# Residual-stream update and its norm statistics moved between engines, and seven PSUM banks in turn, in a two-block transformer kernel

## The reference, cut to what matters

```
for layer in range(DEPTH):
    h = h + 0.5 * rmsnorm_2(swiglu(rmsnorm_2(h, g[0]), ...), g[1])
    hn = rmsnorm_2(h, g[2])
    mix = gla_mixer(hn, ...) or swa_mixer(hn, ...)
    h = h + rmsnorm_2(mix, g[3])
    h = h + 0.5 * rmsnorm_2(swiglu(rmsnorm_2(h, g[4]), ...), g[5])
    if layer == 0: k_sh, v_sh = shared_kv(h, kv_norm, w_kv, cos, sin)
```

## Time and profile before

| | us |
|---|---|
| median of 3 runs | 1949.22 |
| lowest and highest run | 1944.98, 1959.04 |
| profiled execution, its own time | 1958.64 |
| span in its profile | 1956.8 |
| TensorE busy | 1870.8 (96% of the span) |
| VectorE busy | 1270.1 (65%) |
| ScalarE busy | 918.7 (47%) |
| GpSimd busy | 161.6 (8%) |

### The profile page before, as it was taken

The page is one execution under the profiler, slowest core; times in us unless marked ns, Lnnn a source line. Parts: engine busy times, 40 slices in busy tenths (PEclk is TensorE's granted clock), DMA queues, the critical chain, the costliest instruction groups (busy, mean ns, idle before and its releaser), DMA issues.

```text
span 1956.8 us, 33004 instructions
## 1 busy us (share of the span) xinstructions
PE 1870.8 (96%) x13432; PEld 1723.9 (88%) x13432; DVE 1270.1 (65%) x2132; ACT 918.7 (47%) x1581; POOL 161.6 (8%) x204
## 2 busy tenths in 40 slices
PE   6989998999999999999988999999999998999997
PEld 6979996887569998999978878999899996589997
DVE  6867668764467766766565338665776657657664
ACT  7545444442455454544454235444544443445452
POOL 1001005100000001000020022000200011020001
PEclk9999999996799999999998889999999998789999
DMA  4215555530015556555533223555355551125553
GB/s 152 76 41 183 185 187 200 181 134 20 1 44 183 184 189 202 178 175 173 194 108 108 65 76 130 172 173 192 129 187 186 191 183 54 33 87 188 188 194 120
DMA packets 76038, 276.35 MB, mean 141 GB/s; under 512 B 8496, under 2 KB 9520, under 8 KB 75760
## 3 DMA queue, kind: packets, MB, share of 16 engines
q1 hardware_dynamic: 75168, 270.57, 41.3%
q0 software_dynamic: 288, 2.30, 0.4%
q10 hardware_dynamic: 432, 1.38, 0.2%
HBM read 273.16 MB, written 1.05 MB: 140 GB/s over the span
## 4 chain that ended last, share of the span: by engine, by line
PE 86%; DVE 8%; ACT 2%; DMA 2%; issue 1%; POOL 0%; SPq 0%; DVEq 0%; POOLq 0%; ACTq 0%
PE acc L1555 57%; PE acc L1551 5%; PE mix L245 3%; PE mix L1555 2%; PE acc L1552 2%; DMA arrived<-in_w 2%; DVE wl L1794 2%; DVE y L1820 2%; PE acc L632 1%; PE acc L1624 1%; DVE xl L1806 1%; PE acc L1597 1%; PE mix L656 1%; PE acc L1575 1%; PE acc L1047 1%
## 5 line engine op out<-in xcount | busy, mean ns | idle before, releaser
L1794 DVE TENSOR_TENSOR wl<-arrived,wh 128x1024 fp32r<-128x1024 f32 x514 | 641.2, 1248 | 396.7 <-ACT wh L1670 384.6
L1670 ACT ACTIVATE wh<-arrived 128x1024 fp32r<-128x1024 f32 x514 | 541.4, 1058 | 589.0 <-DMA arrived<-in_w 588.5
L1555 PE MATMUL acc<-xh,wh 128*128 128x256 f32 (+1 forms) x2376 | 678.1, 285 | 2.6 <-DVEq L1856 2.2
L1555 PE MATMUL acc<-xh,wl 128*128 128x256 f32 (+1 forms) x2376 | 675.9, 284 | 0.0
L1555 PE MATMUL acc<-xl,wh 128*128 128x256 f32 (+1 forms) x2376 | 675.5, 284 | 0.0
L1555 PEld LDWEIGHTS acc<-xh,wh 128*128 128x128 f32 x2376 | 450.1, 189 | 8.6 <-issue 7.8
L1555 PEld LDWEIGHTS acc<-xh,wl 128*128 128x128 f32 x2376 | 450.5, 190 | 0.0
L1555 PEld LDWEIGHTS acc<-xl,wh 128*128 128x128 f32 x2376 | 448.5, 189 | 0.3
L1555 PE MATMUL acc<-hx,wh 128*128 128x256 f32 (+1 forms) x1664 | 304.1, 284 | 0.0
L1555 PEld LDWEIGHTS acc<-hx,wh 128*128 128x128 f32 x1664 | 258.9, 189 | 0.8 <-issue 0.8
L1555 PE MATMUL acc<-hx,wl 128*128 128x256 f32 (+1 forms) x832 | 236.9, 285 | 0.0
(11 more groups left out here) (387 smaller groups left out, 2225.6 us busy)
## 6 DMA issues: line engine op xcount, KB each, us to landing
arrived<-in_w SPq DMA_DIRECT2D x514, 512.0 KB, 3.3
scr<-in_cmp_w POOLq DMA_DIRECT2D x1, 2048.0 KB, 9.0
x<-in_x ACTq DMA_DIRECT2D x2, 544.0 KB, 8.1
out<-x SPq DMA_DIRECT2D x8, 128.0 KB, 1.7
par<-in_par ACTq DMA_DIRECT2D x1, 259.0 KB, 4.1
scr<-in_positions POOLq DMA_DIRECT2D x1, 128.0 KB, 7.2
scr<-in_cmp_w POOLq DMA_DIRECT2D x1, 32.0 KB, 9.6
scr<-in_w_gate POOLq DMA_DIRECT2D x1, 32.0 KB, 2.7
```

What stands on the lines that cost most here:

```text
L1555: ins = nc.tensor.matmul(bank(name, t)[:, 0:L - c], w_part[:, h.slot, w], v_part[:, k, c:], start=(k == 0 and w_part is wh and v_part is h ...
L1670: nc.scalar.activation(wh[:, h.slot, :], raw(h.slot), ACT.Copy).then_inc(w_hi, 1)
L1794: nc.vector.tensor_tensor(wl[:, h.slot, :], raw(h.slot), wh[:, h.slot, :].bitcast(F32), ALU.subtract).then_inc(w_lo, 1)
```

## The change

- In the second block GpSimd no longer touches `x`. VectorE does all multiplications and additions of the update, in five groups of chunks: two of one chunk and three of two chunks, with the factor `ry` broadcast over the chunks of a group. The order is y0, y1, x0, x1, y23, x23, y45, x45, y67, x67.
- The squares of the new stream are summed by TensorE: eight float32 products `ones`·`sq[k]` that accumulate in `stat`, behind all high products of the opening and ahead of its low products. GpSimd's sum of them and the two-product `mean` in the opening are gone. The sum behind the last output tiles of a stage (for `ry`) stays as it was.
- The last `ahead(b)` of a stage moves: on ScalarE from ahead of the root to behind `xh` and the squares; on VectorE from ahead of `xl` to behind it (at u = 7 between `hl` and `xl`).
- The FFN input stages of both blocks take seven banks in turn, and every wait for a bank is worked out from the bank's last user.

```diff
+GROUPS = ((0, 1), (1, 2), (2, 4), (4, 6), (6, 8))
...
         def bank(name, t):
+            if name.startswith("ffn") and name.endswith("_a"):
+                return (mix + acc)[t % 7]
             if name == "gla_r":
                 return mix[t % 2]
             return mix[2] if name == "swa_q" and t >= 3 else acc[(TILE[name] + t) % 4]
...
+        free_at = []
+        _last = {}
+        for _name, _n in STAGES:
+            for _t in range(_n // KF_PARTS if _name.endswith("_b") else _n):
+                _bank = [b is bank(_name, _t) for b in mix + acc].index(True)
+                free_at.append(_last.get(_bank, 0))
+                _last[_bank] = TILE[_name] + _t + 1
+
+        def bank_free(pe, name, t):
+
+            if free_at[TILE[name] + t]:
+                pe.wait_ge(acc_used, free_at[TILE[name] + t])
...
-            def post_update(u):
-
-                norm_sum(norm_of(u, True), c0(u))
-
-                def add(k):
-                    pool.wait_ge(t_new, 8 * (u - 5) + k + 1)
-                    pool.tensor_tensor(x[:, k, c0(u):], x[:, k, c0(u):], y[:, k, c0(u):], ALU.add).then_inc(x_new[0], 1)
-
-                for k in range(0, KD, 2):
-                    add(k)
-                if u < upto:
-                    norm_sum(norm_of(u), c0(u))
...
                 if u >= 5:
-                    post_update(u)
+                    norm_sum(norm_of(u, True), c0(u))
...
+                if norm is not None:
+                    mean_of_squares(norm_of(norm), c0(norm))
...
-                    if norm is not None and (name, t) == group[1]:
-                        mean(norm_of(norm), c0(norm))
+
+            def mean_of_squares(v, c):
+
+                pe.wait_ge(root_ok, v)
+                for k in range(KD):
+                    pe.wait_ge(sq_new, 8 * v + k + 1)
+                    ins = nc.tensor.matmul(stat[:, 0:L - c], ones[:], sq[:, k, c:], start=(k == 0), stop=(k == KD - 1))
+                ins.then_inc(mean_ok, 1)
...
                     nc.scalar.activation(sq[:, m, c0(u):], bank(name, m)[:, 0:L - c0(u)], ACT.Square).then_inc(sq_new, 1)
-                    ahead(b)
+                    if m < KD - 1:
+                        ahead(b)
...
-                    if u < 5:
-                        ahead(b)
+                    ahead(b)
...
-                for k in range(KD):
-                    scaled(k)
-                    if k:
-                        add(k - 1)
-                add(KD - 1)
+                def scaled(n):
+                    f, e = GROUPS[n]
+                    nc.vector.tensor_tensor(y[:, f:e, c:], y[:, f:e, c:], ry[:, c:].unsqueeze(1).to_broadcast([P, e - f, L - c]),
+                                            ALU.mult).then_inc(t_new, 1)
+
+                def add(n):
+                    f, e = GROUPS[n]
+                    dve.wait_ge(t_new, len(GROUPS) * (u - 5) + n + 1)
+                    nc.vector.tensor_tensor(x[:, f:e, c:], x[:, f:e, c:], y[:, f:e, c:], ALU.add).then_inc(x_sum, 1)
+
+                scaled(0)
+                scaled(1)
+                add(0)
+                add(1)
+                for n in range(2, len(GROUPS)):
+                    scaled(n)
+                    add(n)
+                if u == 7 and u < upto:
+                    for k in range(KD):
+                        kv_low(dve, k)
+                else:
+                    for k in range(KD):
+                        low_x(u, k)
                 ahead(b)
                 if u == 7 and u < upto:
                     for k in range(KD):
-                        kv_low(dve, k)
-                for k in range(KD):
-                    low_x(u, k)
+                        low_x(u, k)
```

More of the change, by code:

```diff
@@ L207, in bank, with stream_new @@
             return mix[2] if name == "swa_q" and t >= 3 else acc[(TILE[name] + t) % 4]
-        def updated(u, k):
-            return 4 * (u - 1) + k // 2 + 1
+        free_at = []
[8 more added lines that the diff above has]
+                pe.wait_ge(acc_used, free_at[TILE[name] + t])
+        def stream_new(eng, u, k):
+            if u < 5:
+                eng.wait_ge(x_new, 8 * (u - 1) + k + 1)
+            else:
+                eng.wait_ge(x_sum, len(GROUPS) * (u - 5) + [n for n, (f, e) in enumerate(GROUPS) if f <= k < e][0] + 1)
         def halved(v):
@@ L1538, in _, with half @@
             pe.wait_ge(const_ok, 7)
-            def half(h, q, name, t, part, hi, lo, c, kt, wait):
+            def half(h, name, t, part, hi, lo, c, kt, wait):
                 pe.wait_ge(w_lo, h.n + 1)
-                if part == 0 and q >= 4:
-                    pe.wait_ge(acc_used, q - (1 if name == "gla_r" else 3))
+                if part == 0:
+                    bank_free(pe, name, t)
                 ks = range(part * KD, min(kt, part * KD + KD))
@@ L1565, in gemm @@
                     for part in range(parts):
-                        half(Half(BASE[name] + t * parts + part), TILE[name] + t, name, t, part, hi, lo, c, kt,
+                        half(Half(BASE[name] + t * parts + part), name, t, part, hi, lo, c, kt,
                              wait if t == 0 else None)
@@ L1679, in high_x @@
                 if u:
-                    act.wait_ge(x_new[k % 2], updated(u, k))
+                    stream_new(act, u, k)
                 else:
@@ L1853, in two @@
                         dve.wait_ge(used, b + 1)
-                        nc.vector.tensor_tensor(tg[:, t, c:], bank(name, 2 * t)[:, 0:L - c], rx[:, c:], ALU.mult).then_inc(f_g, 1)
+                        nc.vector.tensor_tensor(tg[:, t, c:], bank(name, 4 * i + 2 * t)[:, 0:L - c], rx[:, c:], ALU.mult).then_inc(f_g, 1)
                         dve.wait_ge(f_g, n)
@@ L1862, in two @@
                         dve.wait_ge(used, b + 2)
-                        nc.vector.tensor_tensor(tu[:, t, c:], bank(name, 2 * t + 1)[:, 0:L - c], rx[:, c:],
+                        nc.vector.tensor_tensor(tu[:, t, c:], bank(name, 4 * i + 2 * t + 1)[:, 0:L - c], rx[:, c:],
                                                 ALU.mult).then_inc(acc_used, 1)
```

28 lines of the change are left out of this document (10 added, 18 removed).

## The result

| | before | after |
|---|---|---|
| median of 8 runs, us | 1955.85 | 1937.28 |
| lowest and highest run | 1944.98, 1963.04 | 1933.43, 1947.28 |
| profiled execution | 1958.64 | 1938.55 |
| span in its profile | 1956.8 | 1936.8 |
| mean granted clock | 0.951 | 0.954 |

The ratio is 0.9904 with a 95% interval of 0.9876 to 0.9933: 18.6 us less, where the prediction had 22.3 less. Both kernels were run once more later: the changed one took 1938.49 us against 1956.54, ratio 0.9902 (0.988 to 0.9925), and the unchanged kernel beside itself had 0.9998 (0.9977 to 1.002). The prediction had drawn its line for "faster" at one per cent, 19.5 us, and given 0.60 to a gain beyond it; 18.6 us lies just short of that line, and the interval, 0.7 to 1.2 per cent, holds it.

What follows compares the result with a forecast made beforehand. TensorE bounds the kernel, with 86% of the chain. Boundary gains of 5.0 + 3.8 + 2.7 + 7.0 + 3.0 + 0.8 = 22.3 us give 1936.3 profiled, median 1926.9; mechanism 17 to 27 us, range 1914 to 1940.

Steps and rivals of the forecast that it cites:

- rival 1: Behind the openings, half the gain goes back to the weight stream, TensorE waiting at tile 6 or 7; 1938, chance 0.19.
- The opening on TensorE: Second-block openings: high products end at t + 10.05, squares take 3.7 us, low products 4.1, ending at t + 17.85.
- Rival 2: In the openings the clock stays at 0.50, squares and low products costing 7.8 us more each; 1966, chance 0.05.
- at u = 9 [...] the clock never fell: Opening at u = 9, before the change: a slightly shorter thin stretch kept 1.00, supporting full clock in the new openings.
- A double operation: VectorE's update: one operation on two chunks, 544 columns, takes 0.72 us, the next starting after 0.64.
- Rival 3: Slow `y` and `xl` operations have another cause than GpSimd; the last `x` comes 8 us later; 1962, chance 0.02.
- the forecast wait for the late `wl`: Behind the opening at u = 7, the moved split readies the second FFN tile's half late; 1.2 us taken off.
- the half-speed stretch: After u = 5, a stretch of 2.6 us at half speed that may go as well.
- First block: no tile waits for a bank there, so nothing.: In the first block, seven banks were to gain nothing, since no tile there waits for a bank.
- the banks alone are worth almost nothing: At u = 6 and 9, the first tile's bank comes free ahead of t' + 17.85, so seven banks give almost nothing.
- Rival 4: Seven banks make TensorE stumble in FFN input stages, a tenth running at 0.50; 41 us cost, 1968, chance 0.02.
- the first root: At u = 5, the root starts 0.56 us earlier once the weight split ahead of it is removed.

Runs made afterwards that it cites:

- before_again: The kernel before, unchanged, run once more for a second profile; 1957.39 us (12 runs), ratio 0.9998 beside itself.

## Why the prediction was right, and where it was off

The forecast, 17 to 27 us less, holds the 18.6 measured. The time by itself would not decide it: the absolute forecast for the median was 1926.9, rival 1's was 1938, and 1937.28 was measured. What decides are the distances and waits below.

*The opening on TensorE.* Right to 0.1 us in sum: the squares took 3.46 us (3.7 predicted), but they start at t' + 10.13 (10.05) and the low products behind them need 4.2 us (4.1), which brings the first tile to t' + 17.80 (17.85) and t' + 16.8 (16.7). The squares were charged in full, and doubling them and cutting them to one pass both moved the time by that price. Rival 2, the low clock in the opening, is refuted by the 1.00, which all five openings have in both profiles of the changed kernel. One argument against it was weaker than it looked: "at u = 9 [...] the clock never fell" holds for the one execution that was read, and in `before_again` it fell to 0.50 there.

*VectorE.* A double operation takes 0.72 us (0.72 predicted), and the last `x` is there at t' + 5.7 (5.8). The estimate that the prediction worked out from the formula in the Trainium skill (VectorE: DVE Perf Modes, the TRN2 errata) was 724 ns; the trace agrees, with 0.72 us. Rival 3 is refuted by the idle additions and by the squares given back to GpSimd.

*Boundaries.* The moved root comes off one distance and onto the one before it: predicted from `ry` to `ry` are then 4.9, 4.2, 2.3, 7.4, 2.1 and 0.8 us. The first pair has 7.39, 4.26, 2.35, 7.55, 2.07 and 0.71; the second 5.44, 2.98, 2.59, 6.53, 3.53 and 0.78. The opening itself at u = 5 gained 4.40 and 4.64, `rx` at u = 8 came at t' + 11.2 as predicted, and at u = 7 the forecast wait for the late `wl` was 1.2 us and measured 0.89 (3.8 less 1.2 is 2.6, where the prediction wrote 2.7). That the first pair meets u = 9 to 0.1 us is in part luck: the old opening there ran at the full clock in that execution, and in the other one it didn't, which is the 1.5 us between 2.07 and 3.53. At u = 6 it is the other way round, 4.26 and 2.98. What lies beyond 4.9 at u = 5 isn't the half-speed stretch that the prediction hoped to save: the first profile of the changed kernel still has it (clock 0.57 from 1014 to 1018, where the kernel before had 0.65) and has the larger gain; the second hasn't (1.00 from 1012 to 1020) and gains less.

*The term that was wrong: "First block: no tile waits for a bank there, so nothing."* This was a misreading. The waits of the kernel before have, beside the line of the earlier trace rows, another for a bank, at the opening by tiles of the first FFN:

```profile
PE acc L1624 <- DVEq L1897: 1.0, 1, 1.0
```

TensorE stood there 0.99 us, and in that time `xl` gained a lead. With seven banks TensorE starts at once, runs dry and its clock falls to 0.50: about 1 us worse. The other bank step failed too, in the other direction. I said that the banks alone are worth almost nothing; that holds at u = 6 and 9 to 0.01 us, but at u = 7, where the stage in front of the FFN fills the banks and its evacuations wait for `rx`, four banks cost 3.1 us once the opening is fast. In the medians the two and their noise cancel (ratios 0.9902 and 0.9902 to 0.9904). Rival 4 was only half about this; its own mechanism, a clock that swings as banks rotate, is refuted for this kernel: the FFN behind u = 9 has 1.00 over 165 us with seven banks. The Trainium skill (TensorE: Matmul & The Clock Gate, A second HAM failure mode) describes bank cycling in which TensorE goes idle between groups of products; here it was busy 165.00 of the 165 us, so the trace doesn't speak against that page.

*The sum.* 22.3 us predicted, 20.0 and 21.3 by spans, 18.6 and 18.9 by medians. The predicted 1926.9 is lower than 1937.28 mostly because the median of before stood at 1949.2 in three runs and at 1955.9 in eight: 1955.85 − 22.3 would have been 1933.6. The pairs of profiles say where the sum failed: not at the boundaries, where 21.7 us were forecast and 24.3 and 21.9 measured, but ahead of u = 5. There the forecast had 0.56 us less (the first root), and the two pairs have 4.3 and 0.55 us more. The first FFN's opening is 1.6 and 1.4 us of it. In the first pair another 3.1 us lie in the stage of the sparse attention (`rx` to `rx` 230.61 us before, 233.72 after; in the second pair 233.76 and 232.23), whose steps differ from run to run; their cause is open. Rival 1 isn't what happened: at u = 6 and 9 no tile in the 40 us behind the opening waits for its weights, and at u = 7 one does, for 0.89 us.

## What to carry to other kernels

A gain on the critical path is best predicted stage by stage against an event that repeats, here the reciprocals; the stages whose clock steps vary by 3 to 13 us from run to run must be kept out of that sum. Moving work off an engine that slows its neighbour is worth what it unblocks, less what it costs where it goes: the same move was worth 4 to 5.5 us at one boundary and −1.5 us at another, so it should be decided boundary by boundary. More buffers helped here only where the consumer that frees them was itself late; where the producer was late they let the fast engine run dry and cost a clock step. And idle products are no free way to the full clock: on the path of the engine that leads, they cost their own time.

## What the runs showed of the hardware

- VectorE beside GpSimd: an `xl` takes 0.40 us with GpSimd at rest (3.39 us for eight, durations from the first start to the last end) and 0.65 to 0.75 with GpSimd adding (5.30 and 5.97 for eight), also where no data pass between them; an addition of 544 columns goes from 0.72 to 1.04 and 1.19. The Trainium skill (SBUF — State Buffer, SBUF: two separate sides) describes the shared ports as an exclusive lock for the length of an instruction. The rows agree in kind, as the two hold each other up, but they can't show a lock; GpSimd itself took 0.78 to 1.30 us for an addition meanwhile.
- A float32 product of 272 columns costs TensorE 0.46 us and two rows, a float32r one 0.13 us and one row.
- The last part of the window attention, the same instructions in all these kernels, ran at 1.00 in one profile and at 0.50 in the others without idle products: 2.96 us against 5.45 for a round, 106.3 against 119 to 121 for the stage. Bringing it to 1.00 with idle products gave 1.6 us, as they cost 1.9 us a round themselves. Why the clock stayed at 1.00 in that one profile is open.
- A wait of TensorE was followed by a lower clock at two places: 2.45 us in the stretch with 0.74, and 1.52 us for `xl` (at 170.12) in front of the one with 0.65. The second was seen in all eight profiles with seven banks (waits of 1.12 to 1.54 us for `xl`, then 0.50). In the six with four banks TensorE waits 0.87 to 1.39 us for a bank in the same opening, some 5 us earlier, and the clock stays at 1.00. So a wait can cost more than its length, and its length alone doesn't say whether it will.
